# A mixers' value projection by panels of half the input and 512 output features

## The reference, cut to what matters

```python
def mixer_a(h, w_in, v_gain, w_s, b_s, w_out):       # h: 512 x 1024
    proj = h @ w_in                                   # 1024 x 6144
    u = proj[..., :A_WIDTH]                           # A_WIDTH = 2048
    v = rms_norm(proj[..., A_WIDTH:2 * A_WIDTH], v_gain)
    z = proj[..., 2 * A_WIDTH:]
    ...
    mixed = jnp.einsum('gij,bcjgd->bcigd', ws, v) + b_s.T[None, None, :, :, None]
    y = u * mixed * jax.nn.silu(z)
    return y @ w_out
```

## Time and profile before

| | |
|---|---|
| median of 3 runs | 3285.64 us (3284.14 to 3287.79) |
| profiled execution | 3283.43 us, of which the span of the trace is 3281.7 us |
| TensorE (PE) matmul busy | 97% of the span |
| DVE, ScalarE (ACT), GpSimd (POOL) busy | 50%, 34%, 48% |
| mean granted TensorE clock | 0.995 |
| first value matmul and last value matmul, A0 | 32.1 and 134.5 us |
| the same, A3 | 1431.7 and 1529.5 us |

### The profile page before, as it was taken

One profiled execution on the slowest core, in us unless ns is written; L12 is line 12 of the kernel. 1 busy time (PEld: TensorE's weight loads), 2 busy tenths in 40 slices (PEclk: granted clock), 3 DMA queues, 4 the chain that ended last, 5 costly groups with the idle time before them and its releaser, 6 DMA issues.

```text
span 3281.7 us, 39766 instructions
## 1 busy us (share of the span) xinstructions
PE 3196.0 (97%) x16422; PEld 2640.0 (80%) x16422; DVE 1646.3 (50%) x2141; ACT 1101.8 (34%) x1449; POOL 1562.7 (48%) x1138
## 2 busy tenths in 40 slices
PE   8999999999999999999999999999999999999998
PEld 7988878787878888789887877766888777778887
DVE  6753475747474443545536666665212366552223
ACT  3221243434343332332212434444222353232222
POOL 4444475646473454454433511126444566344444
PEclk9999999999999999999999999999999999999999
DMA  5544422211121232245444211112233332122332
GB/s 168 165 160 141 141 101 65 78 65 65 65 77 52 95 98 91 93 144 171 156 143 151 77 39 39 40 38 90 91 102 93 100 128 90 65 65 92 101 96 72
DMA packets 279317, 320.07 MB, mean 98 GB/s; under 512 B 6866, under 2 KB 245089, under 8 KB 278946
## 3 DMA queue, kind: packets, MB, share of 16 engines
q1 hardware_dynamic: 240960, 247.48, 23.5%
q10 hardware_dynamic: 38178, 70.06, 6.3%
HBM read 311.22 MB, written 6.29 MB: 97 GB/s over the span
## 4 chain that ended last, share of the span: by engine, by line
PE 86%; DVE 6%; ACT 3%; POOL 2%; issue 1%; DMA 1%; ACTq 0%; SPq 0%; DVEq 0%; POOLq 0%
PE ps L536 24%; PE ps L538 23%; PE ps L537 23%; PE psx L977 2%; POOL Wl L344 1%; PE psx L743 1%; PE ps L1009 1%; ACT Wh L1225 1%; PE ps L787 1%; PE psx L721 1%; PE psx L536 1%; PE psx L537 1%; PE psx L538 1%; PE psx L760 1%; PE psx L636 1%
## 5 line engine op out<-in xcount | busy, mean ns | idle before, releaser
L344 POOL TENSOR_TENSOR Wl<-Wr,Wh 128x512 fp32r<-128x512 f32 x928 | 1279.5, 1410 | 1521.3 <-ACT Wh L1225 1517.1
L536 PE MATMUL ps<-Ah,Wh 128*128 128x512 f32 x1920 | 772.7, 402 | 6.3 <-POOL Wl L344 6.3
L538 PE MATMUL ps<-Ah,Wl 128*128 128x512 f32 x1920 | 749.2, 390 | 0.0
L537 PE MATMUL ps<-Al,Wh 128*128 128x512 f32 x1920 | 748.5, 390 | 0.0
L1225 ACT ACTIVATE Wh<-Wr 128x2048 fp32r<-128x2048 f32 x232 | 443.0, 1909 | 368.4 <-DMA Wr<-in_w_mlp_in_dram 109.8
L536 PEld LDWEIGHTS ps<-Ah,Wh 128*128 128x128 f32 x1920 | 361.1, 188 | 92.2 <-issue 11.1
L536 PE MATMUL ps<-Yh,Wh 128*128 128x512 f32 x1088 | 425.8, 391 | 4.1 <-issue 2.4
L537 PEld LDWEIGHTS ps<-Al,Wh 128*128 128x128 f32 x1920 | 361.1, 188 | 83.7 <-issue 10.3
L538 PE MATMUL ps<-Yh,Wl 128*128 128x512 f32 x1088 | 424.5, 390 | 0.0
L537 PE MATMUL ps<-Yl,Wh 128*128 128x512 f32 x1088 | 424.5, 390 | 0.0
L538 PEld LDWEIGHTS ps<-Ah,Wl 128*128 128x128 f32 x1920 | 360.7, 188 | 76.6
(11 more groups left out here) (405 smaller groups left out, 4141.5 us busy)
## 6 DMA issues: line engine op xcount, KB each, us to landing
Wr<-in_a_w_in_dram SPq DMA_DIRECT2D x48, 1024.0 KB, 6.7
modw<-in_w_mod_dram ACTq DMA_DIRECT2D x96, 512.0 KB, 5.5
Wr<-in_b_w_in_dram SPq DMA_DIRECT2D x40, 1024.0 KB, 5.1
Wr<-in_w_mlp_in_dram SPq DMA_DIRECT2D x32, 1024.0 KB, 5.6
Wr<-in_w_mlp_out_dram SPq DMA_DIRECT2D x32, 1024.0 KB, 5.2
Wr<-in_a_w_out_dram SPq DMA_DIRECT2D x16, 1024.0 KB, 5.3
Wr<-in_c_w_in_dram SPq DMA_DIRECT2D x16, 1024.0 KB, 5.6
Wr<-in_attn_w_qkv_dram SPq DMA_DIRECT2D x12, 1024.0 KB, 5.2
```

Of the source, the lines that this page charges most:

```text
L344: last = pool.tensor_tensor(E.Wl[:, s, part], E.Wr[:, s, part], E.Wh[:, s, part].bitcast(F32), ALU.subtract)
L536: pe.matmul(o, ah, bh, start=first, stop=False)
L537: pe.matmul(o, ah, bl, start=False, stop=False)
L538: return pe.matmul(o, al, bh, start=False, stop=last)
```

## The change

The values' panels become 4 blocks of k by 512 features: panel (m, h) holds half h of the input for features 512 m to 512 m + 511, in the order (0,0), (0,1), (1,0), ... (3,1). They are still 8 panels of 1 MB. TensorE's new `wide_t` takes for each panel the four position tiles in turn, 12 matmuls of 512 columns each, one PSUM bank to a tile, adding half 1 onto half 0. Squares, copies and sums of squares are over 512 features. `mod_use` and `mod_load` keep their order, four of each to a feature block m. `mod_sum(m-1)` stands after the first tile of panel (m, 0). On ScalarE the split two panels ahead stands before the squares of a block (`ahead(L, "v", m, 1)`) and, for the next, after the last square and ahead of that tile's load.

```diff
@@ panels_of
-    def add(w, k0, n0, *name):
+    def add(w, k0, n0, *name, kt=KD):
         at[name] = len(src)
-        src.append(w.rearrange("(k p) n -> p k n", p=P)[:, k0:k0 + KD, n0:n0 + 256])
+        src.append(w.rearrange("(k p) n -> p k n", p=P)[:, k0:k0 + kt, n0:n0 + 2048 // kt])
-        for n in range(8):
-            add(win, 0, AW + n * 256, L, "v", n)
+        for m in range(4):
+            for h in range(2):
+                add(win, 4 * h, AW + m * 512, L, "v", m, h, kt=4)
@@ pe_program (first_t is taken out)
+    def wide_t(L, p, m, h, between):
+        def triple(t, k, ops):
+            for W, lhs, start, stop in ops:
+                i = pe.matmul(bank[t], lhs[:, 4 * h + k, t * P:(t + 1) * P], part(W, p, k, 0, 512, 4), start=start, stop=stop)
+            return i
         for t in range(TT):
-            into(t)
+            if h == 0:
+                into(t)
+        if m + h == 0:
+            for k in range(4):
+                pe.wait_ge(*A.of("nh", L, k))
+                for t in range(TT):
+                    triple(t, k, [(E.Wh, Ah, k == 0, False), (E.Wl, Ah, False, False)])
+                pe.wait_ge(*h_ready(L)(k))
+                for t in range(TT):
+                    i = triple(t, k, [(E.Wh, Al, False, False)])
+        else:
             for t in range(TT):
+                for k in range(4):
+                    if m == 0 and t == 0:
+                        pe.wait_ge(*h_ready(L)(4 + k))
+                    i = triple(t, k, [(E.Wh, Ah, h + k == 0, False), (E.Wl, Ah, False, False), (E.Wh, Al, False, h == 1 and k == 3)])
+                if h:
+                    i.then_inc(*T.did(L, "v", m, t))
+                    emptied[t] = V.of(L, "v", m, t)
+                if m and h + t == 0:
+                    between(m)
+        if h == 0:
+            i.then_inc(*T.did(L, "vk", m))
@@ pe mixer_a
+        for m_ in range(4):
+            for h in range(2):
+                p = begin(L, "v", m_, h)
+                wide_t(L, p, m_, h, lambda m: mod_sum(m - 1))
                 used(p)
@@ act mixer_a
+        ahead(L, "v", 0, 0)
+        for m in range(4):
+            ahead(L, "v", m, 1)
+            for t in range(TT):
+                n, u = 2 * m + t // 2, t % 2
+                if u == 0 and n < 2:
+                    mod_load(0, 2 * n)
+                if n + u == 0:
+                    mod_load(0, 1)
+                act.wait_ge(*T.of(L, "v", m, t))
+                if m >= 2:
+                    act.wait_ge(*V.of("ss", L, m - 2))
+                if m or t >= 2:
+                    act.wait_ge(*A.of(L, "vq", *((m, t - 2) if t >= 2 else (m - 1, t + 2))))
+                c = 4 + 4 * (m % 2) + t
+                act.activation(sq[:, t % 2, :], ps[t][:], ACT.Square, accum_out=ssA[:, c:c + 1]).then_inc(*A.did(L, "vq", m, t))
+                if t == 3 and m < 3:
+                    ahead(L, "v", m + 1, 0)
                 if n and u == 0:
-                    mod_load(n // 2, 2 * q + 1)
+                    mod_load(n // 2, 2 * (n % 2) + 1)
                 elif 0 < n < 7:
-                    mod_load((n + 1) // 2, 2 * (1 - q))
-            ahead(L, "v", n)
-        act.wait_ge(*V.of("ss", L, 7))
+                    mod_load((n + 1) // 2, 2 * (1 - n % 2))
+        act.wait_ge(*V.of("ss", L, 3))
@@ dve mixer_a
+        for m in range(4):
+            for t in range(TT):
+                n, u = 2 * m + t // 2, t % 2
+                dve.wait_ge(*T.of(L, "v", m, t))
+                dve.wait_ge(*A.of(L, "vq", m, t))
+                dve.tensor_scalar(vA[:, t, m * 512:(m + 1) * 512], ps[t][:], 1.0, None, ALU.mult).then_inc(*V.did(L, "v", m, t))
+                if t == 3:
+                    dve.wait_ge(*(V.of("ss", L, m - 1) if m else V.of("ss0", L)))
+                    c = 4 + 4 * (m % 2)
+                    dve.tensor_tensor(ssA[:, 0:4], ssA[:, 0:4], ssA[:, c:c + 4], ALU.add).then_inc(*V.did("ss", L, m))
                 if n:
-                    mod_use(n // 2, 2 * q + u)
+                    mod_use(n // 2, 2 * (n % 2) + u)
                 elif u:
                     mod_use(0, 0)
                     mod_use(0, 1)
```

More of the change, by code:

```diff
@@ L261, in setting @@
     return E
-def v_bank(n, u):
-    return 2 * u if n == 0 else 2 * ((n + 1) % 2) + u
 D_FIRST = [0, 1, 2, 4, 3, 5, 6, 7]
@@ L365, in mixer_a @@
                            pattern=[[0, 8], [-1, P]], channel_multiplier=1).then_inc(*G.did("cm", L))
-        for n in range(8):
-            ahead(L, "v", n)
+        for m in range(4):
+            for h in range(2):
+                ahead(L, "v", m, h)
         for half in range(2):
@@ L580, in first_f @@
                     emptied[b] = emptied_by[f]
-    def first_t(L, p):
-        for t in range(TT):
-            into(t)
-        for k in range(KD):
-            pe.wait_ge(*A.of("nh", L, k))
-            for t in range(TT):
[L589 to L597, removed]
+    def wide_t(L, p, m, h, between):
[3 more added lines that the diff above has]
+            return i
+        for t in range(TT):
+            if h == 0:
[9 more added lines that the diff above has]
+        else:
+            for t in range(TT):
+                for k in range(4):
[9 more added lines that the diff above has]
+            i.then_inc(*T.did(L, "vk", m))
     def h_ready(L):
@@ L689, in mod_sum @@
                 m.then_inc(*X.did("modsum", L, nb, who))
[L691 to L700, removed]
+        for m_ in range(4):
+            for h in range(2):
+                p = begin(L, "v", m_, h)
+                wide_t(L, p, m_, h, lambda m: mod_sum(m - 1))
+                used(p)
         pe.wait_ge(*G.of("cm", L))
```

## The result

The changed kernel takes 3366.26 us (3363.83 to 3369.65, 3 runs) against 3285.64 before: ratio 1.0252, 95% interval 1.0238 to 1.0266. It is 2.5% slower. The forecast was 3370, range 3338 to 3403, on the slower side with 0.91. Two single executions further down (one of the kernel before, one of experiment 8) took some 4570 us at a mean granted clock of 0.65; they are left out of every median, spread and ratio here.

What follows compares the result with a forecast made beforehand. TensorE, busy 97% of the span, was taken as the bound, with DVE close behind. Stream -15.1, waits +54.4 in A0 and +28.5 in A3, clock +16.1 gave +84: 3370 us, range 3338 to 3403.

Steps and rivals of the forecast that it cites:

- The stream and the small waits: TensorE's value matmuls, bank wait and norm waits in both mixers: 7.9 us less in A0, 7.2 in A3, together 15.1.
- The order on ScalarE: Split ahead of a block's squares waits for its panel: landing 5.4 us, rounding 1.9, so rounded at 7.3.
- The chain in A0: Blocks 1 and 2: last `mod_use` ends 28.7 us after the second panel's start; the sum waits 15.3 us, twice.
- The chain in A3: Blocks 1 and 2: last `mod_use` ends 20.1 us after the second panel's start; the sum waits 6.7 us each.
- the median of 5.5: Upper case: modulation loads of 5.5 us and crowded panels of 6.8 everywhere, waits 65.6 and 47.3: +117, 3403 us.
- The place of the wait: TensorE was to wait at `mod_sum` for the DVE's last modulation step, longest in A0, six times over 6 us.
- with four banks, a tile's bank is wanted again only three tiles later: TensorE's wait for the copy emptying its bank, 1.7 us a mixer, goes: the bank is wanted again after 8.2 us.
- The clock: Granted clock falls to half after seven waits, four in A0 and three in A3, losing 2.3 us each: 16.1 us.
- The sum: Whole kernel: -15.1 + 54.4 + 28.5 + 16.1 = +84 us on the profiled 3283.4, so 3367.4, as median 3370.
- Shallow waits: Rival: panel lands before the first square is due at 2.72 us, so waits stay small: +9, 3295 us; chance 0.07.
- the faster case: Rival: a block's last `mod_use` ends within 2.72 us of its last tile, `mod_sum` never waits: 3270.5 us; chance 0.04.

Runs made afterwards that it cites:

- experiment 8: Kernel before the change, without loads and DVE work of modulation blocks 0 to 3 in both A mixers: 3285.4 us, ratio 1.0004.
- 7: Changed kernel with banks waited for tile by tile, without loads and DVE work of modulation blocks 0 to 3 in both A mixers: 3271.86 us, ratio 0.9964.
- experiment 1: Changed kernel, but ScalarE rounds both panels of a block after its last square: 3311.45 us, ratio 1.0079.
- Experiment 2: Changed kernel, but a block's first panel waits for each tile's bank just ahead of that tile: 3374.77 us, ratio 1.0272.
- Experiments 4: Changed kernel with rounding after squares, banks tile by tile, sum after the next block's fourth tile; run twice: 3281.29 and 3281.00 us.
- experiment 11: Changed kernel: rounding after squares, banks tile by tile, sum after next block's fifth tile, block 0's copies 2 and 3 before modulation steps: 3280.38 us.
- experiment 12: Changed kernel with banks waited for tile by tile, plus 50 (A0) or 42 (A3) constant matmuls before each of six sums: 3367.38 us, ratio 1.0249.
- experiment 5: Changed kernel with 42 unused matmuls of 128 columns before each of the six waits for the banks: 3363.91 us, ratio 1.0237.

## Why the prediction was right, point by point

**The stream and the small waits**: forecast -15.1 us, measured -13.5 by 7 against 8. Gaps of 227 against 120 ns carry most of it. By the gap of N/2.4 + 2.5 ns that the Trainium skill gives in "TensorE: Matmul & The Clock Gate", Part 2, it would have been 7 us, an estimate. No run here agrees with that: the measured difference is about twice as much.

**The order on ScalarE**: right, to the tenth. The first square stands 7.3 us after the start of the block's second panel (5.45 for the landing and 1.9 for the rounding, with 5.4 and 1.9 forecast), and experiment 1 gives 55 us back for moving it (with the sum where it is; 21 when it stands three tiles later).

**The chain in A0**: forecast 28.7 us to the block's end, measured 107.5 - 80.7 = 26.8. The third call of `mod_use` ran before GpSimd's split, not beside it. In block 0 the steps end at 71.0 us, 27.9 after the start of the block's second panel, with 29.9 forecast.

**The chain in A3**: forecast 20.1, measured 1544.1 - 1519.8 = 24.3. This term was too small. I gave every modulation load 4.2 us, the value of a quiet stretch; here the loads took 5.3 and 4.5, so that the next split on GpSimd started ahead of the last steps, which then took 3.5 us instead of 1.3. It is the row with the median of 5.5 that holds in this place.

**The place of the wait was wrong.** The step "with four banks, a tile's bank is wanted again only three tiles later" failed. `wide_t` waits for all four banks ahead of its first tile, and the diff shows it. So TensorE waits for the copy of tile 3 first, 60.8 us in six, and hardly at all in front of the sums (2.4 us in three), where I had put six waits of 6.7 to 16.5 us. Experiment 2 shows that for the time it makes little difference (8 us more without the bank wait, of some 80), since both end at the same chain on the DVE; it makes a large one for whoever reads the wait rows.

**The clock**: forecast 7 x 2.3 = 16 us. The falls are there, as far as 0.50, but a part of each lies in the tile in front of the sums, when the modulation is late in any case. What is paid, by the positions in the trace, is about 3.5 us in the later tiles of A0 (twice 9.9 against 8.16), 1 in each of three blocks of A3, and 1.5 and 2.2 at the z stages of A0 and A3, some 10 us. In A0's first block nothing is paid: its slow first tile ends at 70.5, and the last `macc` step of the DVE, which the sums need, at 70.4. The fall at A3's z stage was not among the forecast's seven. Had I walked through the restart tile by tile as I did for the DVE, this would have come out.

**The sum.** A0 was forecast at +56 (46.5 and four restarts) and is +42.0; A3 was forecast at +28 and is +33.5; about 5 us came from elsewhere, and not from the edit. Block by block, each with its restart, the delays (before the stream's gain is taken off) were forecast at 19, 18, 18 and 10 us in A0 and are about 14, 15, 15 and 8; in A3 at 14, 9, 9 and 3, and are about 12, 12, 11 and 6. The errors have opposite signs: that forecast and result lie only 4 us apart is in part luck. Both main causes were the right ones, and each is shown by a run of its own.

**The rivals.** Shallow waits (+9) needed the panel to land ahead of the first tile's end; it took 5.45 us against 2.72. Experiments 4 and 11 made the condition of the faster case nearly true by other orders, and reached 3281 and 3280, where 3270.5 was its price; only some of their executions (3268 to 3273 us) do.

## What to carry to other kernels

When a product is tiled so that its results come in a burst, look at what is interleaved with each result: here four modulation steps, each a transfer, a wait and some vector work, went with four tiles that used to come in 23 us and now come in 11. A wait for a transfer at the head of an in-order engine's program holds all that the engine could already do; it belongs behind the work that is ready. And the row with the most waiting need not be the one to mend: see first what would be waited for next.

## What the runs showed of the hardware that I had not expected

- The granted clock fell although the gap had been filled: after matmuls without a pause until about 110 us, a wait of 1.8 us and 16 single-column matmuls brought it from 1.00 to 0.50 within 4 us (experiment 12), and likewise in experiment 5. In the changed kernel it fell twice in one block. In the kernel before, the same 16 single-column matmuls, with no wait ahead and dense work on both sides, left it at 1.00. Behind filling that left no wait, in A3, 8 of them left it at 1.00 as well. So the single-column matmuls alone did not do it in these places; what they add to a wait was not separated.
- The executions of 4 and 11 spread over 17 to 21 us, those of the same tiling without the modulation over 2.3. The time goes with the mean granted clock of the execution: of experiment 11's twelve, five lie at 3268.1 to 3273.4 us with 0.995 or 0.996, seven at 3278.0 to 3288.8 with 0.990 to 0.992. The two profiled executions of 4 (spans 3280.2 and 3272.2 us, clock 0.992 and 0.995) differ by 3.3 us up to A0's sum 3, by 1.5 from there to A3, and by 3.2 behind A3's sum 3. Why the clock falls more often in one execution than in another stays open.
